# Turning the experts' rows by halves on two row tiles of the array

## The reference, cut to what matters

```python
def expert_block(args):                  # first block
    xb, e = args
    hb = jax.nn.silu(xb @ w_gate[e]) * (xb @ w_up[e])
    return hb @ w_down[e]

def block_ffn(args):                     # second block
    xb, e = args
    return (jax.nn.silu(xb @ w_gate[e]) * (xb @ w_up[e])) @ w_down[e]
```

## Time and profile before

| | |
|---|---|
| Median of 3 runs | 3456.67 us (3455.22 to 3461.14) |
| The profiled execution's own time | 3455.7 us |
| Its span | 3454.0 us |
| TensorE matmul busy | 3156.8 us (91%) |
| VectorE / ScalarE / GpSimd busy | 45% / 21% / 20% |
| Mean granted TensorE clock | 0.957 of 2.4 GHz |
| DMA moved | 564.84 MB, mean 164 GB/s |

### The profile page before, as it was taken

How to read it: one execution, slowest core, us unless ns; L and a number is a source line. 1 busy time by engine, 2 the same in 40 slices (tenths; PEclk the granted TensorE clock), 3 DMA queues, 4 the chain that set the end, 5 groups by cost and what they waited for, 6 DMA issues and landing times. The chain is left out here.

```text
span 3454.0 us, 46196 instructions
## 1 busy us (share of the span) xinstructions
PE 3156.8 (91%) x14927; PEld 1544.3 (45%) x14928; DVE 1567.1 (45%) x2431; ACT 727.7 (21%) x1169; POOL 703.4 (20%) x917
## 2 busy tenths in 40 slices
PE   8999989987999996789969998988999999999992
PEld 4444445544665444333337773444333333333330
DVE  3322234446775123434456675344444444444444
ACT  2222223343543001011123330211011111111112
POOL 1000000000000000334510000000455545555552
PEclk9999999998999997899979998999999999999996
DMA  6201021124231124799740111221888998898885
GB/s 230 98 30 43 0 85 50 54 68 95 52 96 50 30 112 195 270 386 384 267 156 25 34 30 49 83 95 65 305 273 274 350 331 293 292 300 277 272 263 181
DMA packets 180326, 564.84 MB, mean 164 GB/s; under 512 B 18684, under 2 KB 93024, under 8 KB 143072
## 3 DMA queue, kind: packets, MB, share of 16 engines
q1 hardware_dynamic: 142864, 429.69, 32.9%
q0 software_dynamic: 34128, 127.45, 15.0%
q10 hardware_dynamic: 3240, 6.45, 0.5%
HBM read 460.27 MB, written 103.27 MB: 163 GB/s over the span
## 5 line engine op out<-in xcount | busy, mean ns | idle before, releaser
L1894 PE MATMUL gu_ps<-w_gu,second 128*64 x1648 | 741.2, 603 | 13.8 <-DVE second L1988 8.6
L1897 PE MATMUL gu_ps<-h,second 128*64 128x512 f32 x1648 | 741.2, 603 | 0.0
L1894 PEld LDWEIGHTS gu_ps<-w_gu,second 128*64 128x64 f32 x1648 | 220.1, 139 | 448.1 <-issue 436.5
L1919 PE MATMUL y_ps<-w_dn,hid_t 128*64 x824 | 379.1, 603 | 11.6 <-issue 8.7
L1922 PE MATMUL y_ps<-second,hid_t 128*64 128x512 f32 x824 | 379.1, 603 | 0.0
L1522 POOL COPY moe_idx<-moe_slot_tok 128x1 int32<-128x1 int32 x4 | 0.6, 183 | 1811.0 <-DVEq L1457 1225.0
L355 PE MATMUL front<-second,wcol 128*128 128x512 f32 x768 | 332.1, 595 | 4.8 <-ACTq L63 2.4
L1964 DVE COPY h<-w_gu 128x4096 f32 x109 | 249.6, 2290 | 96.2 <-SPq L1771 96.0
L1848 POOL DMA_INDIRECT token_sums<-second,idx_y x103 | 243.3, 2362 | 18.0 <-issue 16.9
L355 PEld LDWEIGHTS front<-second,wcol 128*128 128x128 f32 x768 | 146.4, 191 | 189.6 <-issue 189.6
L1897 PEld LDWEIGHTS gu_ps<-h,second 128*64 128x64 f32 x1648 | 220.1, 139 | 0.0
(11 more groups left out here) (453 smaller groups left out, 4780.1 us busy)
## 6 DMA issues: line engine op xcount, KB each, us to landing
w_gu<-in_w_gate_dram SPq DMA_DIRECT2D x96, 1024.0 KB, 12.8
w_gu<-in_w_up_dram SPq DMA_DIRECT2D x96, 1024.0 KB, 15.8
w_dn<-in_w_down_dram SPq DMA_DIRECT2D x96, 1024.0 KB, 10.5
wcol<-in_w_in_dram SPq DMA_DIRECT2D x12, 1024.0 KB, 5.4
qk_by_head<-stage SPq DMA_DIRECT2D x32, 384.0 KB, 3.7
qk<-qk_by_head SPq DMA_DIRECT2D x16, 768.0 KB
w_gu<-in_w_in_dram SPq DMA_DIRECT2D x20, 512.0 KB, 5.0
token_sums<-zero POOLq DMA_DIRECT2D x19, 512.0 KB, 12.6
```

What stands on the lines that cost most here:

```text
L1894: nc.tensor.matmul(gu_ps[0:PART, slot], x_t[:, slot, c, 0:PART], w_gu[:, bass.ds(ws, 1), :, c, :].rearrange("p o g n -> p (o g) n"), start ...
L1897: last = nc.tensor.matmul(gu_ps[PART:P, slot], x_t[:, slot, c, PART:P], st_gu[:, slot, :, c, :], start=c == 0, stop=c == C - 1)
L1919: nc.tensor.matmul(y_ps[0:PART, cs], hid_t[:, c, 0:PART], w_dn[:, bass.ds(ws, 1), c, cs].rearrange("p o n -> p (o n)"), start=c == 0, stop ...
```

## The change

The transposes are done by halves of 64 rows. Each transpose of 128 x 128 becomes two: one that takes the rows 0 to 63 of the source as weights (64 rows by 128 columns) and streams the 64 x 64 corner of the identity, and one that does so with the rows 64 to 127. The first lies on the array's rows 0 to 63, the second on its rows 64 to 127: two row tiles of 64 x 128. Their results, 128 partitions x 64 columns each, go to two different PSUM banks: `x_ps` keeps its two banks but they now hold one half each, and `h_ps` takes two banks where it took one. The three VectorE copies read the halves and write them back into the old layout of `x_t` and `hid_t`. A semaphore `turn_go` is added that nobody waits for; TensorE adds to it ahead of each turn, so that the wait for the rows (or for `hid`) rides on that addition and no longer on the first transpose.

```diff
+def turn_rows_by_half(nc, G, out, src):
+
+    for a in range(2):
+        rows = slice(a * PART, (a + 1) * PART)
+        last = nc.tensor.transpose(out[:, a], src[rows, :], G.ident[rows, rows])
+    return last
...
-        x_ps = ph.ps("x_ps", [P, C, P])
+        x_ps = ph.ps("x_ps", [P, 2, C, PART])
         gu_ps = ph.ps("gu_ps", [P, 2, 2, F_EXP])
-        h_ps = ph.ps("h_ps", [P, BANK // P, P])[:, 0:FC, :]
+        h_ps = ph.ps("h_ps", [P, 2, BANK])[:, :, 0:FC * PART].rearrange("p a (c n) -> p a c n", c=FC)
...
             def turn_rows(b, slot, landed):
                 pe.wait_ge(x_in[slot], landed)
+                pe.sem_inc(turn_go, 1)
                 for c in range(C):
-                    last = nc.tensor.transpose(x_ps[:, c, :], xb[:, slot, c:D:C], G.ident[:])
+                    last = turn_rows_by_half(nc, G, x_ps[:, :, c, :], xb[:, slot, c:D:C])
                 last.then_inc(x_turned, 1)
...
                 pe.wait_ge(hid_ready, i + 1)
+                pe.sem_inc(turn_go, 1)
                 for c in range(FC):
-                    last = nc.tensor.transpose(h_ps[:, c, :], hid[:, slot, c::FC], G.ident[:])
+                    last = turn_rows_by_half(nc, G, h_ps[:, :, c, :], hid[:, slot, c::FC])
                 last.then_inc(h_turned, 1)
...
-                d.tensor_copy(x_t[:, 1 - slot], x_ps[:]).then_inc(x_ready, 1)
+                d.tensor_copy(x_t[:, 1 - slot].rearrange("p c (a n) -> p a c n", a=2), x_ps[:]).then_inc(x_ready, 1)
                 v.wait_ge(h_turned, i + 1)
-                d.tensor_copy(hid_t[:], h_ps).then_inc(h_ready, 1)
+                d.tensor_copy(hid_t[:].rearrange("p c (a n) -> p a c n", a=2), h_ps).then_inc(h_ready, 1)
```

More of the change, by code:

```diff
@@ L1742, in experts @@
         y = work[:, 4 * D:6 * D].rearrange("p (s n) -> p s n", s=2)
-        x_ps = ph.ps("x_ps", [P, C, P])
+        x_ps = ph.ps("x_ps", [P, 2, C, PART])
         gu_ps = ph.ps("gu_ps", [P, 2, 2, F_EXP])
-        h_ps = ph.ps("h_ps", [P, BANK // P, P])[:, 0:FC, :]
+        h_ps = ph.ps("h_ps", [P, 2, BANK])[:, :, 0:FC * PART].rearrange("p a (c n) -> p a c n", c=FC)
         y_ps = ph.ps("y_ps", [P, D])
         (g_ready, d_ready, g_staged, d_staged, idx_ready, idx_y_ready, x_turned, x_ready, gu_ready,
-         silu_done, hid_ready, h_turned, h_ready, y_ready, share_in, share_ready, y_taken, y_out0, y_out1) = ph.sems(
+         silu_done, hid_ready, h_turned, h_ready, y_ready, share_in, share_ready, y_taken, y_out0, y_out1, turn_go) = ph.sems(
             "g_ready d_ready g_staged d_staged idx_ready idx_y_ready x_turned x_ready gu_ready "
-            "silu_done hid_ready h_turned h_ready y_ready share_in share_ready y_taken y_out0 y_out1")
+            "silu_done hid_ready h_turned h_ready y_ready share_in share_ready y_taken y_out0 y_out1 turn_go")
         x_in, y_out = G.xb_in, [y_out0, y_out1]
@@ L1987, in _ @@
             v.wait_ge(x_turned, 1)
-            d.tensor_copy(x_t[:, 0], x_ps[:]).then_inc(x_ready, 1)
+            d.tensor_copy(x_t[:, 0].rearrange("p c (a n) -> p a c n", a=2), x_ps[:]).then_inc(x_ready, 1)
             stage_gate_up(1, 1)
```

## The result

The changed kernel takes 3561.05 us (median of 4 runs, 3558.81 to 3565.69) against 3455.94 us before: ratio 1.0305, 95% interval 1.0287 to 1.0323. The forecast was 3449.6 us with a range of 3410 to 3540, so both the sign and the range were missed. The profiled execution took 3565.7 us with a span of 3564.0.

What follows compares the result with a forecast made beforehand. TensorE was taken to bound the second call and weight loads the first. From 3455.7 us, 7.1 us for shorter turns gave 3448.6; with 1.0 us for the median, 3449.6 us, range 3410 to 3540.

Steps and rivals of the forecast that it cites:

- What bounds the kernel: In `experts`, weight loads set the pace of the first call and TensorE that of the second, where its microseconds count fully.
- The turns: Transposes of token rows and `hid` in the second call: 0.09 us saved per block, 7.1 us over 79 blocks.
- the turn is halved: Rival for the transposes: half-transpose pairs follow each other by 0.0575 us, saving 43 us, to 3413.7 us; chance 0.16.
- The rival on the slower side: Loads of the two row tiles go one behind the other: 79 us more, 3535.7 us; chance 0.25.
- the semaphore addition and what is queued there: TensorE's addition ahead of each turn, with the wait moved onto it and the instructions queued behind: costed at nothing.
- upper bound of 14 us: Most the semaphore addition could cost, from 0.09 us at a change of shape, two turns per block, 79 blocks.
- First call: Its 24 blocks would gain 2.2 us, but the loads hold it, so nothing was taken.
- VectorE's copies: Copies of the transposed halves: even half as long again they stay under VectorE's 2.83 us idle time, so cost nothing.

Runs made afterwards that it cites:

- a_hoist: The changed kernel with TensorE's sequencer reading the expert number ahead of the token rows' turn, not behind it: 3449.47 us against 3457.59, ratio 0.9975.

## Why the prediction was wrong

**What bounds the kernel: right.** The second call is TensorE's, and the loss is there: from its first turn to its last it takes 1065.0 us where it took 960.4.

**The turns: right, slightly under.** Row tiles load side by side, a pair each 0.11 us, held by the strided load, and only the ends get shorter. I took 0.09 us per block; a_hoist's block of the second call takes 12.01 us where it took 12.12, 0.11 less. Over 79 blocks that is 8.7 us against my 7.1, and the measured gain of a_hoist is 8.1. The rival "the turn is halved" was wrong for strided rows. With neighbouring ones a turn takes 0.64 us, near the 0.6 that it gave, and for the reason it was weighed by.

**The rival on the slower side: wrong in its mechanism.** The loads do not go one behind the other (16 of them in 0.96 us). That its 3535.7 us lies near the measured time is chance.

**The step that failed** is the one on the semaphore addition and what is queued there: "So I cost the addition at nothing", with the reason that the pairs of 512 columns "give the sequencer time to run ahead". The addition itself does cost nothing that can be seen: a_hoist keeps both of a block and is faster than the kernel before. I looked only at it and its wait. I did not ask what doubling the instructions of the turn does to the instructions behind it: the read of `moe_blk_e`, which stands in the order shown ahead of the prediction right behind `x_ps ... x16`. With 16 instructions of the turn (8 loads, 8 matmuls) the sequencer got past them while gate and up matmuls ran, with 32 it does not. My upper bound of 14 us was for the addition. The late read made the way from a turn's start to the first down pair 82 us longer over the second call, and 27 us more went to down matmuls at the lower clock, a consequence that had no term at all. Both halves of this were to be had in the trace of before: the read stood only 1.6 us ahead of the turn in the block of the earlier trace rows, and the like read of L1888, behind the start of the turn, took 0.59 us and not 0.30.

**First call: right.** There the read is late too but quick (0.30 to 0.38 us in all 24 blocks but one), and the weights' loads hide it: from first to last turn the call takes 317.9 us, before 319.8.

**VectorE's copies: right.** Nothing waits for them but once, 1.1 us.

## What to carry to other kernels

Splitting instructions on TensorE is not only a matter of the array's time: count the instructions between the last long matmul and the next thing that the sequencer itself must do. Here it was a register read: behind 16 instructions it hid, behind 32 it did not. Waits and address steps alone were not tried. Put such reads ahead of a burst of short instructions. And before halving a transpose by rows, look at how long its load takes: with strided rows the load of all columns holds it (1.03 us per turn for 1.08), with neighbouring ones the halves pay (0.64 us for 1.02).

## What the runs showed of the hardware that was not expected

- TensorE's sequencer reads one number from on-chip memory in 0.30 us as a rule. Beside the transfers of the indirect scatters that add, it takes 0.96 to 1.62 us (73 reads of the changed kernel's second call, all but the last at the start of the token rows' turn), and 0.59 us in the median when it starts 1.4 to 1.9 us behind that start (L1888 before). Beside the gathers on the same queue it takes 0.30 to 0.33 us, as it does beside the loads of weights that fill the DMA engines.
- Loads of a transpose of 128 columns take 193 ns with every eighth element (halves 199), 204 to 206 with every second and 141 to 143 with neighbours; two row tiles load at the same time.
- The idle gaps behind the changed kernel's turns are mostly of two lengths, 0.8 to 1.0 us (36 blocks of the second call) and 1.3 to 1.5 us (34). Behind 16 of the long ones the granted clock fell to 0.50 for the next four pairs, 1.7 us more each; behind the shorter ones it never did. From 2603 us on it is nearly every second long gap. Why not every one stays open.
- How many instructions TensorE's sequencer can be ahead is not settled. With 16 in the turn the read starts 1.8 us ahead of the turn in the median and at most 2.7, with 32 at 0.02 to 0.16 us behind its start; nothing in between was run. Who counts from the list ahead of the prediction should know that the trace has 16 pairs of gate and up matmuls in a block (1648 / 103), not 8.
